# Bank of the first expert's gather, place of two transposes, and order of two splits in a two-block fp32 network on one core

## What is computed

```python
def _moe(h, w_router, b_router, wg, wu, wd):
    logits = (t @ w_router).astype(jnp.float32) + b_router
    top_v, top_i = lax.top_k(logits, TOP_K)
    ...
    for e in range(N_EXPERTS):
        out = out + gates[:, e:e + 1].astype(t.dtype) * _swiglu(t, wg[e], wu[e], wd[e])

def second_block(x, mem, ...):
    for l in range(DEPTH):
        h = rmsnorm(x, norm_mix[l])
        p = h @ w_in[l] + b_in[l]
        ...
        x = x + cross_attention(rmsnorm(x, norm_x[l]), rmsnorm(mem, norm_mem[l]),
                                xa_wq[l], xa_wk[l], xa_wv[l], xa_wo[l])
```

## Time and profile before

| | |
|---|---|
| median of 3 runs | 2784.83 us (2782.84 to 2785.06) |
| profiled execution, and its span | 2773.45 us, 2771.6 us |
| PE busy | 2663.4 us, 96% |
| PE weight loads busy | 2363.7 us, 85% |
| DVE busy | 2196.3 us, 79% |
| ACT busy | 1520.4 us, 55% |
| mean granted clock of PE | 0.972 |
| bytes moved | 669.86 MB, mean 242 GB/s |

### The profile page before, as it was taken

The page is one execution under the profiler, slowest core; times in us unless marked ns, Lnnn a source line. Parts: engine busy times, 40 slices in busy tenths (PEclk is TensorE's granted clock), DMA queues, the critical chain, the costliest instruction groups (busy, mean ns, idle before and its releaser), DMA issues.

```text
span 2771.6 us, 37886 instructions
## 1 busy us (share of the span) xinstructions
PE 2663.4 (96%) x15712; PEld 2363.7 (85%) x15712; DVE 2196.3 (79%) x2513; ACT 1520.4 (55%) x1567; POOL 50.1 (2%) x83
## 2 busy tenths in 40 slices
PE   6889999979999999999999989999999999999998
PEld 5778998768888888888888779999899999998898
DVE  7877777768888898988888878895487789954777
ACT  3424345437767777677777755544455564444554
POOL 2000000000000000000000000000000000000000
PEclk9879999999999999999999999999999999999999
DMA  8739875269999999999999943446355543544453
GB/s 311 250 129 339 321 250 175 96 198 363 349 356 349 349 360 347 360 347 357 349 360 345 365 157 106 134 152 210 127 199 183 174 149 115 168 152 154 166 183 114
DMA packets 376065, 669.86 MB, mean 242 GB/s; under 512 B 26825, under 2 KB 199503, under 8 KB 371023
## 3 DMA queue, kind: packets, MB, share of 16 engines
q1 hardware_dynamic: 358400, 662.55, 68.0%
q10 hardware_dynamic: 17487, 4.83, 0.7%
HBM read 663.13 MB, written 4.19 MB: 241 GB/s over the span
## 4 chain that ended last, share of the span: by engine, by line
PE 85%; DVE 9%; ACT 2%; issue 1%; DMA 1%; POOL 0%; ACTq 0%; DVEq 0%; POOLq 0%
PE PS L444 24%; PE PS L446 24%; PE PS L445 24%; PE PS L544 2%; DVE LO L439 2%; PE PS L1629 2%; PE PS L2464 2%; DVE AR L2753 1%; DMA RAW<-in_w_ada_dram 1%; PE PS L1860 1%; ACT HI L430 1%; PE PS L2350 1%; PE PS L1896 1%; DVE RAW L697 1%; DVE AR L697 1%
## 5 line engine op out<-in xcount | busy, mean ns | idle before, releaser
L439 DVE TENSOR_TENSOR LO<-RAW,HI 128x2048 fp32r<-128x2048 f32 x410 | 930.7, 2275 | 238.0 <-ACT HI L430 237.9
L430 ACT ACTIVATE HI<-RAW 128x2048 fp32r<-128x2048 f32 x410 | 780.2, 1904 | 351.2 <-PE PS L446 307.2
L444 PE MATMUL PS<-X1H,HI 128*128 128x256 f32 (+1 forms) x2128 | 610.7, 287 | 10.6 <-DVE X1L L584 4.8
L445 PE MATMUL PS<-X1L,HI 128*128 128x256 f32 (+1 forms) x2128 | 604.5, 284 | 0.0
L446 PE MATMUL PS<-X1H,LO 128*128 128x256 f32 (+1 forms) x2128 | 604.4, 284 | 0.0
L444 PE MATMUL PS<-HI,X1H 128*128 128x512 f32 x1056 | 431.1, 408 | 3.5 <-DVE LO L439 3.5
L444 PEld LDWEIGHTS PS<-X1H,HI 128*128 128x128 f32 (+1 forms) x2128 | 408.8, 192 | 15.8 <-issue 8.6
L446 PE MATMUL PS<-HI,X1L 128*128 128x512 f32 x1056 | 414.0, 392 | 0.0
L445 PE MATMUL PS<-LO,X1H 128*128 128x512 f32 x1056 | 413.0, 391 | 0.0
L445 PEld LDWEIGHTS PS<-X1L,HI 128*128 128x128 f32 (+1 forms) x2128 | 408.9, 192 | 2.0
L446 PEld LDWEIGHTS PS<-X1H,LO 128*128 128x128 f32 (+1 forms) x2128 | 408.7, 192 | 0.7
(11 more groups left out here) (392 smaller groups left out, 2891.9 us busy)
## 6 DMA issues: line engine op xcount, KB each, us to landing
RAW<-in_w_in_dram SPq DMA_DIRECT2D x66, 1024.0 KB, 5.2
RAW<-in_expert_w_gate_dram SPq DMA_DIRECT2D x66, 1024.0 KB, 5.2
RAW<-in_expert_w_up_dram SPq DMA_DIRECT2D x64, 1024.0 KB, 5.2
RAW<-in_expert_w_down_dram SPq DMA_DIRECT2D x62, 1024.0 KB, 5.4
RAW<-in_ffn_w_up_dram SPq DMA_DIRECT2D x55, 1024.0 KB, 5.6
AR<-in_expert_w_down_dram SPq DMA_DIRECT2D x50, 1024.0 KB, 5.4
AR<-in_expert_w_up_dram SPq DMA_DIRECT2D x48, 1024.0 KB, 5.5
AR<-in_expert_w_gate_dram SPq DMA_DIRECT2D x46, 1024.0 KB, 5.3
```

The lines of the kernel that those rows point to most:

```text
L430: a.activation(HI[:, n % NH, 0:size(i)], raw_at(i), ACT.Copy).then_inc(*hi.up(i))
L439: v.tensor_tensor(LO[:, m % NH, 0:n], raw_at(i), HI[:, m % NH, 0:n].bitcast(F32), ALU.subtract).then_inc(*lo.up(i))
L444: t.matmul(o, lh, rh, start=first, stop=False)
L445: t.matmul(o, lh, rl, start=False, stop=False)
```

## The change

- The second half of the first expert's gather goes to bank 4 and its turn to bank 6. Neither waits for a half to be read any more. The second expert's gather waits for the read of the first's half 0 instead of the copy of its turn.
- In block 1 the transpose of the hidden block 0 stands behind g1(1) instead of g0(1).
- On DVE, in block 55, one split (d0(55)) stands behind "hid" of block 55 instead of ahead of it.
- On ACT, the split of in20m[1] stands in layer two, behind the copy and the store of the first keys and ahead of the squares, instead of ahead of the scaling of the memory's columns.

```diff
+    def gather_bank(x, half):
+        return 4 if x == 0 and half else 7
+
     def pe_gather(t, x, half):
         if half:
-            t.wait_ge(*dve_moe("gather", x, 0))
+            if x:
+                t.wait_ge(*dve_moe("gather", x, 0))
         elif x > 1:
             t.wait_ge(*dve_moe("scatter", x - 2, 3))
         elif x == 1:
-            t.wait_ge(*act_moe("turn", 0))
+            t.wait_ge(*dve_moe("gather", 0, 0))
...
     def pe_turn(t, x):
-        t.wait_ge(*dve_moe("gather", x, 1))
-        turn(t, [(PS[:, 7, 128 * k:128 * k + 128], PG[:, x % 2, k, :]) for k in range(2)]).then_inc(*pe_moe.up("turn", x))
+        if x:
+            t.wait_ge(*dve_moe("gather", x, 1))
+        turn(t, [(PS[:, 7 if x else 6, 128 * k:128 * k + 128], PG[:, x % 2, k, :]) for k in range(2)]).then_inc(*pe_moe.up("turn", x))
...
-                    if q == 0 and k == 0 and n > 0:
+                    if q == 0 and n > 0 and k == (n == 1):
                         pe_turn_hidden(t, n - 1)
...
             if n == 55:
                 act_hidden_moe(a, 55)
-            if n > 0:
+            if 0 < n < 56:
                 split_hi(a)
-            if 0 < n < 56:
                 split_hi(a)
         act_memory_cols(a, "experts", 0, raw[slot_of[CH["mf"][1]]](CH["mf"][1]), raw_cols(CH["mf"][1]))
...
                 split_lo(v)
                 dve_between(v, x, b, "g")
                 split_lo(v)
-                split_lo(v)
+                if n < 55:
+                    split_lo(v)
                 v.wait_ge(*act_moe("silu", n))
...
             if n == 55:
+                split_lo(v)
                 dve_hidden_moe(v, 55)
...
         if l == 0:
             act_early(a, 1, 4)
             act_early_out(a, 1)
+            split_hi(a)
         act_squares(a, X, xn, lambda q: dve_two("ffnx", q, 0) if l else dve_res("x", 1, 1, q), "mix", l)
```

More of the change, by code:

```diff
@@ L1859, in pe_gather @@
             for k in range(2):
-                z = t.matmul(PS[:, 7, 128 * c:128 * c + 128], HM[:, k, 512 * half + 128 * c:512 * half + 128 * c + 128],
+                z = t.matmul(PS[:, gather_bank(x, half), 128 * c:128 * c + 128], HM[:, k, 512 * half + 128 * c:512 * half + 128 * c + 128],
                              PP[:, x % 2, k, :], start=(k == 0), stop=(k == 1))
@@ L1867, in act_gather @@
             a.wait_ge(*used(CH[f"moe{x - 2}u"][13]))
-        a.activation(GH[:, x % 2, 4 * half:4 * half + 4, :], PS[:, 7, :].rearrange("p (c n) -> p c n", c=4),
+        a.activation(GH[:, x % 2, 4 * half:4 * half + 4, :], PS[:, gather_bank(x, half), :].rearrange("p (c n) -> p c n", c=4),
                      ACT.Copy).then_inc(*act_moe.up("gather", x, half))
@@ L1873, in dve_gather @@
         v.wait_ge(*act_moe("gather", x, half))
-        v.tensor_tensor(GL[:, x % 2, 4 * half:4 * half + 4, :], PS[:, 7, :].rearrange("p (c n) -> p c n", c=4),
+        v.tensor_tensor(GL[:, x % 2, 4 * half:4 * half + 4, :], PS[:, gather_bank(x, half), :].rearrange("p (c n) -> p c n", c=4),
                         gh.bitcast(F32), ALU.subtract).then_inc(*dve_moe.up("gather", x, half))
     def pe_turn(t, x):
-        t.wait_ge(*dve_moe("gather", x, 1))
-        turn(t, [(PS[:, 7, 128 * k:128 * k + 128], PG[:, x % 2, k, :]) for k in range(2)]).then_inc(*pe_moe.up("turn", x))
+        if x:
+            t.wait_ge(*dve_moe("gather", x, 1))
+        turn(t, [(PS[:, 7 if x else 6, 128 * k:128 * k + 128], PG[:, x % 2, k, :]) for k in range(2)]).then_inc(*pe_moe.up("turn", x))
     def act_turn(a, x):
@@ L1884, in act_turn @@
             a.wait_ge(*pe_moe("scatter", x - 2, 3))
-        a.activation(PGT[:, x % 2, :], PS[:, 7, 0:256], ACT.Copy).then_inc(*act_moe.up("turn", x))
+        a.activation(PGT[:, x % 2, :], PS[:, 7 if x else 6, 0:256], ACT.Copy).then_inc(*act_moe.up("turn", x))
     def scatter_bank(x, q):
```

## The result

| | before | after |
|---|---|---|
| median of 4 runs, us | 2784.21 (2782.84 to 2785.06) | 2763.86 (2762.56 to 2766.13) |
| ratio, 95% interval | | 0.9928 (0.9911 to 0.9945) |
| profiled execution, and its span, us | 2773.45, 2771.6 | 2762.56, 2760.8 |
| start of the first gather, us | 595.18 | 598.05 |
| from there to layer two's first product, us | 1036.05 | 1022.32 |

The change makes the kernel 20.0 us faster (2784.21 x (1 - 0.9928); 15.3 to 24.8 by the interval).

A forecast was written before the change was run, and what follows sets the result against it. PE bounds the expert blocks (busy 967.72 of 970 us), and the order of its work costs. Gains of 2.7 + 2.7 + 8.4 = 13.8 us, taken from the median 2784.83, gave 2771.0 us, range 2765 to 2778.

The forecast's parts named there:

- Part 1: First gather: with separate banks its second half and turn follow without waits; gain 2.7 us, bounds 1.1 to 2.8.
- late clock: Rival at the first gather: second half wholly at 1.2 GHz, gain 1.1 us instead of 2.7; 2772.6 us, chance 0.14.
- Part 2: First hidden transpose, block 1: one more product fills PE's 2.76 us wait; gain 2.7 us.
- the 0.4 us that I saw to spare: Behind the first hidden transpose: d0(0)'s splits ready after 5.5 us, PE having 5.9 us of work until then.
- The lead lasts: Expert blocks: the 5.4 us won at the start stay, as loads keep over 7 us to spare.
- the rival of the eaten lead: Expert blocks: PE waits for loads until the 5.4 us are gone; 2776.4 us, chance 0.09.
- Part 3: Last hidden transpose, block 55: with the split behind the hidden product it starts earlier; gain 2.4 us.
- Part 4: End of experts: memory columns scaled earlier, keys products follow the scatter at full clock; 8.4 us together with Part 3.
- the rival on the slower side: Layer two: the moved split waits for its load and delays all behind it; 0.2% slower at 2790 us, chance 0.03.
- the last one of the sum: Whole kernel: the 13.8 us gain, as stalls of fixed length, subtracted unscaled from the median 2784.83, giving 2771.0 us.
- some us for clock dips in layer two: Layer two: clock dips falling elsewhere, allowed for only in the range, within 2765 to 2775 us.
- D: Later theory of the missing 6 us: timed executions lose clock ahead of the first gather or behind layer two's first product.

The follow-up runs named there:

- shift6: The kernel before with six extra comparisons in the router, ahead of the first gather; ratio to before 0.9995 (0.9980 to 1.0010).
- r_after: The changed kernel, unchanged, run again on another chip beside the kernel before; 2762.93 us, ratio 0.9925.
- shifted traces: Traces of the kernel before with three, six or nine extra comparisons in the router; ratios 1.0003, 0.9995 and 1.0003.
- p12: The kernel before with only the gather banks and the later first hidden transpose changed; 2772.38 us, ratio 0.9954.
- warm: The kernel before, order and waits kept, with unread products of constants in PE's idle time at the edited places; 2774.38 us, ratio 0.9967.

## Why the prediction was right and where it was wrong

**Part 1: right, a little more than forecast.** From the gather's start to the first product it is 603.73 - 598.05 = 5.68, against 604.03 - 595.18 = 8.85: 3.2 us, forecast 2.7. The clock rose about when I took it to: both halves together took 5.37 to 6.24 in six traces with separate banks, where I had 3.78 + 0.30 + 1.89 = 5.97. The late clock, which I had as a rival to the gain, struck the order that is removed: shift6's second half ran for 3.78 behind its 1.41 of idling.

The Trainium skill ("TensorE: Matmul & The Clock Gate", Part 1: The HAM clock gate) says that the moment of the rise is free-running and differs from run to run. The traces agree: the same 16 products took 2.05 in before and 3.78 in shift6, which differs ahead of them by six comparisons. I had weighed this at one place, and only against the change. With before's order the time at half clock varies from trace to trace behind each of its idle spells, and that spoke for the change.

**Part 2: right.** From the first product to the first hidden transpose it is 16.62 before and 16.70 after, with one more product of 2.73 in it; the wait is gone. No LO came late: PE goes on without a wait, and the 0.4 us that I saw to spare sufficed.

**The lead lasts: right.** No load held ACT in the blocks, and PE was busy 970.00 of 970. From the first to the last hidden transpose it is 973.77 before and 968.47 after, 5.3 less: the product that left this stretch (2.73) and part 3. That rules out the rival of the eaten lead.

**Part 3: right.** The wait of 2.28 is gone, and the splits behind it came in time.

**Part 4: right, with 0.5 us lost on the way.** The keys follow the scatter without a wait and take 13.98, forecast 14.14. From the scatter's start to layer two's first product it is 26.97 before and 21.11 after: 5.9 us, forecast 8.4 - 2.4 = 6.0. The last hidden transpose to the scatter grew from 9.84 to 10.36, which I hadn't seen coming (9.89 in r_after, so it isn't always so). PE idles 1.04 ahead of layer two's transposes, forecast 0.7. The moved split waits for no load: the rival on the slower side had no ground.

**The time: wrong by 7 us, and the step that failed is the last one of the sum.** "The median of the runs shown is 2784.83, 11.4 (0.4%) above it; the gain is in stalls of fixed length, so I subtract it unscaled". The waits are of fixed length, in the shifted traces too; their price is not. It was the length alone in the one execution that I read, which had lost no clock behind the gather's idle spells and behind the two hidden transposes; I charged such a loss at the keys alone, where the trace showed it (1.63). In the shifted traces and in p12's PE runs at half clock behind one or more of the other spells too, and the edits take that away with the spells. No execution of before that took the median time was traced; that its clock falls there as well rests on these traces, on warm's 9.2 us and on the clocks listed for the runs. I had seen that the profiled execution was 11.4 us below the median and passed over it. It was the sign: what an execution in the median has, and this one hasn't, has to be somewhere, and if it comes of the stalls, it goes with them. Instead I gave the clock only "some us for clock dips in layer two", in the range and not in the sum.

How far this accounts for the difference can be added up in two ways. By the traces: the edited stretch takes 1039.5 to 1040.4 in the three shifted kernels with before's order and 1022.0 to 1022.3 in the three with the new one, 17.1 to 18.2 at the same shift, not 13.7. In these traces the clock lost in that stretch, summed from the granted clock, is 9.0 to 9.6 us in the one group and 1.8 to 2.5 in the other, some 7 apart (before 3.8, after 2.0). By the granted clock of the timed runs: the mean listed for the runs of before beside r_after is 0.9693, which over its time is (1 - 0.9693) x 2783.6 = 85 us short of full clock; for r_after it is 0.9714, 79 us. The profiled executions of before had 0.972 and 0.973. So some 6.5 us of lost clock went with the change, as an estimate. Of the 13.7 in the two profiles 15.77 - 13.98 = 1.8 were such lost clock already, at the keys; the lengths are 11.9, and 11.9 + 6.5 = 18.4, near the first way. (This takes each us at half clock as half a us lost, so it is an estimate; where PE idles at half clock, nothing is lost.)

**What stays open.** Both ways leave 2 to 3 us of the 20 unplaced. The front (the first gather starts at 595.2 to 600.4 where no comparisons are added) and all behind layer two's first product (1139.4 to 1146.8) vary between executions of the same code, at places that the change doesn't touch; of that much D is right. The second of these goes with the clock too: it took 1139.4 to 1140.5 us where the granted clock shows 17.3 to 17.8 us lost in it, and 1145.3 to 1146.8 where it shows 22.6 to 24.3. It was over 1145 in four of nine traces with before's keys order and in none of six with the new one, and its mean is 1142.9 and 1140.9, about what is unplaced; that can be chance, and nothing here tells whether it is.

## What to carry to other kernels

A stall of PE costs its length and, in some executions, half clock behind it. When the profiled execution lies well below the median of the runs, ask what it lacks before adding up stalls from it; a second trace, with all of the work moved by some us, shows this cheaply. And to price the clock apart from the wait, fill the idle time with products that nobody reads: what is won then is the clock alone, and where the order can't be mended, it is a gain to take (9.2 us here, of the 20 that the better order brings).

## What the runs showed of the hardware that was not expected

- Idle spells of 2.27 us, all alike, in an otherwise busy PE were followed by a granted clock of 0.50 in 23 of 55 cases. One fall cost 1.3 us by the timed runs and 1.6 by the traces; the granted clock came back while PE was busy. Fills of 1.88 us in each such spell left 1.00 throughout.
- Executions of one unchanged kernel spread over 10 us and more (2774.5 to 2789.0 in 17 runs), and the listed clock mostly goes with it: the profiled ones of before at 2773.5 had 0.972 and 0.973, the runs beside r_after 0.9693 in the mean at 2783.6.
- The Trainium skill (same page and section) puts the ramp penalty at under 1% of a typical kernel's span and advises not to fit it to a count of slow products. In the trace of before PE is busy for about 128 us at a granted clock of 0.50, which costs some 64 us, 2.3% of the span (an estimate: half of that busy time); for this kernel the measurement decides. The part that the change removes, 6.5 us, is 0.2% of the span, but a third of what this change brings.
